# LayerNorm 1 of a decoder layer with features on the partitions, its input and W_out centred beforehand, its sum of squares by products with ones

## The reference, cut to what matters

```python
proj = x @ w_in                      # 1024 -> 512 pooling + 4 x 512 mLSTM + 8 gates
y_pool = ...                         # trailing-window pooling mixer
h, C1, n1, m1 = _mlstm(q, k, v, ig, fg, C, n, m)
y_ml = sigmoid(o_pre) * h
mix = concatenate([y_pool, y_ml], axis=-1) @ w_out
x1 = _layer_norm(ALPHA * x + mix, ln1_g, ln1_b)
ff = square(relu(x1 @ w_ff1 + b_ff1)) @ w_ff2 + b_ff2
x2 = _layer_norm(ALPHA * x1 + ff, ln2_g, ln2_b)

def _layer_norm(x, g, b):
    mu = mean(x, axis=-1)
    xc = x - mu
    var = mean(xc * xc, axis=-1)
    return xc * rsqrt(var + LN_EPS) * g + b
```

## Time and profile before

| | us |
|---|---|
| median of 3 runs | 1066.43 (1066.04 to 1066.63) |
| profiled execution, its span | 1064.2 |
| TensorE busy in it | 1053.9 |
| DVE busy | 724.6 |
| ACT busy | 500.3 |
| GpSimd busy | 92.3 |

### The profile page before, as it was taken

One profiled execution on the slowest core, in us unless ns is written; L12 is line 12 of the kernel. 1 busy time (PEld: TensorE's weight loads), 2 busy tenths in 40 slices (PEclk: granted clock), 3 DMA queues, 4 the chain that ended last, 5 costly groups with the idle time before them and its releaser, 6 DMA issues. The chain is left out here.

```text
span 1064.2 us, 19251 instructions
## 1 busy us (share of the span) xinstructions
PE 1053.9 (99%) x7935; PEld 1042.0 (98%) x7935; DVE 724.6 (68%) x989; ACT 500.3 (47%) x733; POOL 92.3 (9%) x119
## 2 busy tenths in 40 slices
PE   9999999999999999999999999999999999999996
PEld 9999999999899999999999999999999999999985
DVE  6795555537789864955555555558767577788977
ACT  6453535442554666654555545556452322334223
POOL 3010000020212320000000000000000000000027
PEclk9999999999999999999999999999999999999999
DMA  8502222362154841235435534568623525435304
GB/s 283 147 4 60 63 60 63 92 175 79 47 200 127 259 126 46 80 120 170 150 119 159 158 119 154 163 221 275 239 81 139 170 71 167 132 91 169 120 9 151
DMA packets 97394, 139.88 MB, mean 131 GB/s; under 512 B 5963, under 2 KB 56875, under 8 KB 96934
## 3 DMA queue, kind: packets, MB, share of 16 engines
q1 hardware_dynamic: 93728, 127.65, 37.9%
q0 software_dynamic: 3328, 10.77, 3.6%
q10 hardware_dynamic: 270, 0.49, 0.2%
HBM read 102.75 MB, written 36.38 MB: 131 GB/s over the span
## 5 line engine op out<-in xcount | busy, mean ns | idle before, releaser
L2201 PE MATMUL bank<-x_hi,w_hi 128*128 128x344 f32 (+1 forms) x696 | 228.1, 328 | 0.0
L2201 PE MATMUL bank<-x_hi,d_lo 128*128 128x258 f32 x968 | 222.4, 282 | 0.0
L2201 PE MATMUL bank<-x_lo,w_hi 128*128 128x344 f32 (+1 forms) x696 | 222.0, 319 | 0.0
L2201 PE MATMUL bank<-x_hi,w_lo 128*128 128x344 f32 x528 | 168.8, 320 | 0.0
L2201 PEld LDWEIGHTS bank<-x_hi,d_lo 128*128 128x128 f32 x968 | 165.7, 189 | 0.0
L2201 PEld LDWEIGHTS bank<-x_hi,w_hi 128*128 128x128 f32 (+1 forms) x696 | 130.4, 187 | 0.1
L2201 PEld LDWEIGHTS bank<-x_lo,w_hi 128*128 128x128 f32 (+1 forms) x696 | 130.3, 187 | 0.1
L2201 PE MATMUL bank<-x_lo,s_hi 128*128 128x258 f32 x448 | 126.5, 282 | 0.0
L2201 PE MATMUL bank<-x_hi,s_hi 128*128 128x258 f32 x448 | 126.4, 282 | 0.0
L2201 PEld LDWEIGHTS bank<-x_hi,w_lo 128*128 128x128 f32 x528 | 99.2, 188 | 0.0
L2201 PE MATMUL bank<-t_hi,s_hi 128*128 128x258 f32 x336 | 95.2, 283 | 0.0
(11 more groups left out here) (391 smaller groups left out, 2485.2 us busy)
## 6 DMA issues: line engine op xcount, KB each, us to landing
h_ops<-h_unit SPq DMA_DIRECT2D x56, 258.0 KB, 2.8
x_lo_raw<-h_ops SPq DMA_DIRECT2D x14, 1032.0 KB, 5.3
s_raw<-in_w_ff SPq DMA_DIRECT2D x14, 1024.0 KB, 7.0
w_raw<-in_w_out SPq DMA_DIRECT2D x12, 1024.0 KB, 6.9
x_lo_raw<-h_ops SPq DMA_DIRECT2D x14, 774.0 KB, 4.5
d_raw<-in_w_ff SPq DMA_DIRECT2D x9, 1024.0 KB, 7.8
w_raw<-in_w_in SPq DMA_DIRECT2D x16, 512.0 KB, 6.2
h_ops<-t_out SPq DMA_DIRECT2D x28, 258.0 KB, 5.0
```

The costliest lines, as they stand in the source:

```text
L2201: return nc.tensor.matmul(out, lhsT, rhs, start=start, stop=stop, skip_group_check=True)
```

## The change

Let xc be x minus its mean over the features, and Wc be W_out with the mean of each row, over the output features, taken off. Then ALPHA * xc + h @ Wc equals ALPHA * x + h @ W_out minus its own mean. The change computes that sum, so that the mean of LayerNorm 1 is zero, and keeps features on the partitions throughout.

- **The mean of x.** A column of −1/1024 is put into the padding of the gate product, whose row 68 then holds minus the mean of each token. SP writes it to DRAM (`nm_d`).
- **x centred in DRAM** (`xt_d`). SP writes the high parts of x at units 4 and 5. GpSimd adds the low parts at pairs 7 and 8, and minus the mean in eight broadcasts at pairs 10 and 11; these DMAs add to what is in DRAM. SP loads each row of 128 features (`load_xt`) in the output stage.
- **W_out centred.** GpSimd loads W_out's rows at pairs 2 to 5, two of 128x1024 at a time; DVE sums each along its row (`w_out_rows`, in four pairs, at units 4 and 5). ACT adds minus the mean to each quarter of W_out before its split (`centre`, eight instructions a quarter).
- **Order of the output products** (`OUT_ORDER`, written (j, b)). Each quarter of W_out is loaded and split once. The 24 products are numbered p, two for each entry.
- **The residual** (`residual(p)`): DVE adds ALPHA times xc while it evacuates the product, in place of ACT's copy.
- **The variance.** ACT squares a block's outputs (six, then two chunks), TensorE makes eight fp32 products of a matrix of ones with the squares (`square_sums(b)`), which gives the sum on all partitions. ACT takes the root, DVE the reciprocal and two multiplications over 4x344, ACT scales and shifts and makes the high part in two halves, DVE the low parts.
- `mix_T`, `norm_T`, `norm1`, `ln1_a`, `ln1_b`, `x1_T`, `mix_evac` and GpSimd's nine loads of x by tokens are gone.

The diff, without the removed functions, which the listing above shows:

```diff
-U_FFN = U_OUT + NBLK * (D // UW)
+U_FFN = U_OUT + D // UW
+OUT_ORDER = [(0, 0), (1, 0), (0, 1), (1, 1), (0, 2), (1, 2), (2, 0), (3, 0), (2, 1), (3, 1), (2, 2), (3, 2)]
...
+                if u == 3:
+                    sp.wait_ge(x_hi, 2 * len(XT) + 1 + NBLK)
+                    sp.dma_start(nm_d, GL[NH:NH + 1, 0, :]).then_inc(nm_out, 16)
                 if u >= 3:
                     load_rows(u - 3)
+                if u == 4:
+                    sp.dma_start(xt_d[:, 4:8, :], XH[:, 4:8, :].bitcast(F32)).then_inc(xt_hi, 16)
+                elif u == 5:
+                    for b in (0, 2):
+                        sp.dma_start(xt_d[:, 0:4, blk(b)], XH[:, 0:4, blk(b)].bitcast(F32)).then_inc(xt_hi, 16)
+                    sp.wait_ge(b12_out, 48)
+                    sp.dma_start(xt_d[:, 0:4, blk(1)], b12_d[0]).then_inc(xt_hi, 16)
...
+            def load_xt(m):
+                if m == 0:
+                    sp.wait_ge(xt_done, XT_DONE)
+                    sp.wait_ge(pooled, 4)
+                elif m == 1:
+                    sp.wait_ge(sn_out, 16)
+                elif m == 2:
+                    sp.wait_ge(E_ready, 2 * NPAIR)
+                    sp.wait_ge(qi_ready, NPAIR)
+                elif m == 3:
+                    sp.wait_ge(mixed, 12)
+                else:
+                    sp.wait_ge(gemm_read, outputs_of(m - 4, m - 3, NBLK - 1))
+                sp.dma_start(XTM[:, 3 - m % 4, :], xt_d[:, m, :]).then_inc(xt_in[m % 4], 16)
...
+                    p = PAIRS * h + j
+                    if 2 <= p < 6:
+                        if p == 2:
+                            pool.wait_ge(dve_row, ROW_RX)
+                            pool.wait_ge(act_row, 6)
+                        else:
+                            pool.wait_ge(wr_sum, 2 * (p - 2))
+                        for x in range(2):
+                            k = 2 * (p - 2) + x
+                            pool.dma_start(WR[x][:, :], a["w_out"][0, P * k:P * (k + 1), :]).then_inc(wr_in, 16)
+                    elif p == 7:
+                        pool.wait_ge(xt_hi, XT0 + 64)
+                        pool.dma_start(xt_d[:, 4:8, :], XL[:, 4:8, :].bitcast(F32), max_dma_last_dim=4 * NT, accum_op=ALU.add).then_inc(xt_done, 16)
+                    elif p == 8:
+                        for b in (0, 2):
+                            pool.dma_start(xt_d[:, 0:4, blk(b)], XL[:, 0:4, blk(b)].bitcast(F32), max_dma_last_dim=4 * NT, accum_op=ALU.add).then_inc(xt_done, 16)
+                        pool.dma_start(xt_d[:, 0:4, blk(1)], b12_d[1], max_dma_last_dim=4 * NT, accum_op=ALU.add).then_inc(xt_done, 16)
+                    elif p in (10, 11):
+                        if p == 10:
+                            pool.wait_ge(nm_out, NM0 + 16)
+                            pool.wait_ge(xt_done, XT_LO)
+                        for k in range(4 * (p - 10), 4 * (p - 10) + 4):
+                            pool.dma_start(xt_d[:, k, :], nm_d.to_broadcast([P, NT]), max_dma_last_dim=4 * NT, accum_op=ALU.add).then_inc(xt_done, 16)
...
+            def centre(j):
+
+                u = U_OUT + j
+                act.wait_ge(raw_in[u % 2], RAW_AT[u])
+                if j == 0:
+                    act.wait_ge(wr_sum, KC + 1)
+                for k in range(KC):
+                    A(wslot(RAW, u)[:, k, :], wslot(RAW, u)[:, k, :], ACT.Identity, bias=WM[:, k:k + 1]).then_inc(w_centred, 1)
...
+            def square(b, last):
+                m0, m1 = (6, 8) if last else (0, 6)
+                act.wait_ge(gemm_read, outputs_of(m0, m1, b))
+                if not last:
+                    if b == 0:
+                        act.wait_ge(c_out, 128)
+                    else:
+                        act.wait_ge(var_ready, VAR0 + b)
+                A(SQ[:, m0:m1, :], Y[:, m0:m1, blk(b)], ACT.Square).then_inc(squared, 1)
+
+            def root(b):
+                act.wait_ge(var_ready, VAR0 + b + 1)
+                if b:
+                    act.wait_ge(ln_norm, 2 * b)
+                A(RSTD[:, :], D_[:, 0:BLK], ACT.Sqrt, scale=1.0 / D, bias=EPSC).then_inc(ln_sqrt, 1)
...
+            def x1_half(b, h):
+                act.wait_ge(ln_norm, 2 * b + h + 1)
+                ks = slice(4 * h, 4 * h + 4)
+                for f in range(4 * h, 4 * h + 4):
+                    A(Y[:, f, blk(b)], Y[:, f, blk(b)], ACT.Identity,
                       scale=CST[:, G1 + f:G1 + f + 1], bias=CST[:, B1 + f:B1 + f + 1]).then_inc(xv_ready, 1)
+                act.wait_ge(xv_ready, KC * b + 4 * h + 4)
+                A(XH[:, ks, blk(b)], Y[:, ks, blk(b)], ACT.Copy).then_inc(x1_hi, 1)
+
+            square(0, False)
+            square(0, True)
+            root(0)
+            square(1, False)
+            x1_half(0, 0)
+            x1_half(0, 1)
+            square(1, True)
+            root(1)
+            ffn_hi(0)
+            square(2, False)
+            x1_half(1, 0)
+            square(2, True)
+            ffn_hi(1)
+            root(2)
+            x1_half(1, 1)
...
+            def w_out_rows(u, i):
+                if u in (4, 5) and i in (2, 5):
+                    for x in range(2):
+                        k = 4 * (u - 4) + 2 * (i // 3) + x
+                        dve.wait_ge(wr_in, 32 * (k // 2 + 1))
+                        V.tensor_reduce(WM[:, k:k + 1], WR[x][:, :], AX.X, ALU.add).then_inc(wr_sum, 1)
+                    if (u, i) == (5, 5):
+                        dve.wait_ge(wr_sum, KC)
+                        V.tensor_scalar(WM[:, :], WM[:, :], -1.0 / D, None, ALU.mult).then_inc(wr_sum, 1)
...
+            def residual(p):
+                j, b = OUT_ORDER[p // 2]
+                m, n = 2 * j + p % 2, N_PROJ + p
+                dve.wait_ge(gemm_done, n + 1)
+                if b == 0:
+                    dve.wait_ge(xt_in[m % 4], XT0 + 16 * (m // 4 + 1))
+                stt(Y[:, m, blk(b)], XTM[:, 3 - m % 4, blk(b)], ALPHA, bank[n % 3][:, 0:BLK], ALU.mult, ALU.add)\
+                    .then_inc(gemm_read, 1)
...
+            def r_std(b):
+                dve.wait_ge(ln_sqrt, b + 1)
+                V.reciprocal(RSTD[:, :], RSTD[:, :]).then_inc(ln_rstd, 1)
+
+            def normed(b, h):
+                dve.wait_ge(ln_rstd, RSTD0 + b + 1)
+                r = Y[:, 4 * h:4 * h + 4, blk(b)]
+                V.tensor_tensor(r, r, over_blocks(RSTD[:, :], 4), ALU.mult).then_inc(ln_norm, 1)
+
+            def x1_lo_half(b, h):
+                dve.wait_ge(x1_hi, 2 * b + h + 1)
+                ks = slice(4 * h, 4 * h + 4)
+                V.tensor_tensor(XL[:, ks, blk(b)], Y[:, ks, blk(b)], XH[:, ks, blk(b)].bitcast(F32),
...
+            residual(5)
+            cat_lo_part(2, False)
+            residual(6)
+            sample_rows()
+            residual(7)
+            cat_lo_part(2, True)
+            residual(8)
+            new_C(0)
+            residual(9)
+            split_lo(U_OUT + 2)
+            residual(10)
+            new_C(1)
+            residual(11)
+            split_lo(U_OUT + 3)
+            residual(12)
+            residual(13)
+            residual(14)
+            residual(15)
+            residual(16)
+            r_std(0)
+            residual(17)
+            normed(0, 0)
+            normed(0, 1)
+            residual(18)
+            residual(19)
+            x1_lo_half(0, 0)
+            residual(20)
+            x1_lo_half(0, 1)
+            r_std(1)
+            residual(21)
+            normed(1, 0)
+            normed(1, 1)
+            ffn_lo(0)
+            residual(22)
+            residual(23)
+            x1_lo_half(1, 0)
...
+            def square_sums(b):
+                pe.wait_ge(squared, SQ0 + 2 * b + 2)
+                if b:
+                    pe.wait_ge(ln_sqrt, b)
+                else:
+                    pe.wait_ge(nat_read, 2)
+                for m in range(KC):
+                    last = mm(D_[:, 0:BLK], ONES[:, :], SQ[:, m, :], m == 0, m == KC - 1)
+                last.then_inc(var_ready, 1)
...
+                elif p == 16:
+                    square_sums(0)
+                elif p == 20:
+                    square_sums(1)
...
+                if i == 0:
+                    square_sums(2)
```

More of the change, by code:

```diff
@@ L189, in build_layer @@
         o_xn = o_fa + 2 * XROW + 4 * HALF * 4
-        XN = at("x_nat", [P, 2, D], o_xn)
-        RS = at("res_nat", [P, 2, D], o_xn + 8192)
+        XTM = at("x_T_centred", [P, 4, NT], R["h_blk"])
+        SQ = at("squares", [P, KC, BLK], R["qkv0"] - 3 * XROW)
+        RSTD = at("r_std", [P, BLK], R["sample_C"])
+        WR = [at(f"w_out_rows{x}", [P, D], o_r1 + (6 + x) * XROW) for x in range(2)]
         o_top = [o_r2, o_r2 + 2 * TOP, o_xn]
@@ L1762, in variance, with scale_and_shift @@
                 V.tensor_scalar(L[:, 14:15], L[:, 13:14], EPS, None, ALU.add).then_inc(stats, 1)
-            def scale_and_shift(t, sqrt_done, numbers, tiles=TILES):
+            def scale_and_shift(t, sqrt_done, numbers, tiles):
                 L = LNT[0:tiles[t][1], t % 3, :]
```

(55 more changed lines are left out.)

245 lines of the change are left out of this document (71 added, 174 removed).

## The result

The changed kernel takes 1081.67 us in the median (1079.02 to 1082.21, 4 runs) against 1066.51 of before (4 runs, one more than in the table above): a ratio of 1.0139, 95% interval 1.0124 to 1.0153. The forecast was 1066.9, its range 1064.9 to 1071.9. The profiled execution is the one of 1081.15 us, with a span of 1079.4, 15.2 more than the earlier trace rows.

A forecast was written before the change was run, and what follows sets the result against it. TensorE, busy for 1053.9 of 1064.2 us, was taken as the bound. The terms −0.7 + 0.4 + 0.3 + 0.5 = +0.5 gave a span of about 1064.7 and a time of 1066.9 us, range 1064.9 to 1071.9.

The forecast's parts named there:

- rival C: Slower: the accumulating transfers of x and the mean's broadcasts could delay a weight transfer by some us; about 1070, chance 0.04.
- TensorE's own account: Output product and LayerNorm 1: 15.0 us off for removed transposes, 14.3 on for ones products; −0.7, between −1.0 and −0.3.
- p = 8: First product of the output stage's third block: TensorE waits for the last low parts, +0.4 us (0.2 to 0.6).
- Row sums of W_out: Vector-engine reductions, units 4 and 5: +0.3 us (0 to 0.6) for both pairs, +0.5 (0 to 6) for late rows.
- Rival A: Slower: W_out's rows land late in unit 4, holding the vector engine and TensorE; 1072.4 at 13.9 us landing, chance 0.14.
- The chain of LayerNorm 1: Squares, root, reciprocal, scale and shift have cover and cost nothing; margin 1.3 us at the second block's squares.
- Rival B: Slower: LayerNorm 1's scale and shift take 0.8 instead of 0.46 each, so squares come late; about 1069.5, chance 0.08.
- Rival D: Faster: ones products run like split ones, 0.157 each, 3.8 instead of 14.3 us; time 1056.4, chance 0.03.

## Why the prediction was wrong, step by step

**The step that failed is rival C.** It said of the adding transfers that "they would have to be 60 us late to be waited for; their load could delay a weight transfer by some us", gave about 1070 and a chance of 0.04; the sum itself has no term for these transfers at all. The first half asks when the transfers' own result is read, and is true, though the second four were issued at 218 us and not by 215. The second half was left as a guess, though the trace of before could have answered it: which loads are issued in that stretch, after how long do they land, and how long after their issue are they needed. The reload of x_lo had 19 us from issue to its use and took 6.1; the last w_in load was issued at 222.35, just as the engines became 0.88 busy, and the scalar engine reached its split 14.5 us later:

```profile
236.83 1.91 ACT L807 ACTIVATE w_hi<-w_raw 128x2048 fp32r<-128x2048 f32 x1
```

It then took 5.2 to land, and 28.5 with the broadcasts in front. The price was 15 us (10.2 idle, 4.4 slow clock), nearly five times the 3 that I gave. The trace of before shows these covers, but not how late a load would be; that the range should have reached past 1080 is hindsight.

**The clock.** I priced each stall at its own length. Here each of the two idle stretches of 5.8 and 4.4 us was followed by 4.0 and 4.8 us at the 1.2 GHz level, which added 4.4 to 10.2. That was not in the sum. Shorter stalls did not pay it: the one of 1.3 us in the run with pairs 8 and 9, and one of 1.9 us at 167 us in the run with pairs 7 and 8, left the granted clock of their stretches at 1.00. Between 1.9 and 4.4 us nothing was measured.

**TensorE's own account: right in kind, some tenths too small.** −15.0 and +14.3 gave −0.7. The ones blocks cost 4.6 each, 13.9 in all; the earlier trace rows gave 4.8 each. In the run with the late broadcasts TensorE is busy for 1053.0 us against 1053.9; by the account below it is about −1.4.

**p = 8: right.** 0.4 was forecast; the changed kernel's timeline has 0.22 of idle time:

```profile
334.64 0.43 PE L2315 MATMUL bank<-x_hi,w_hi 128*128 128x344 f32 x1 [0.22 <-DVE x_lo L1612]
```

Idle time counts from the end of the matmul before, whose record lasts 0.32 while the next one normally starts after 0.16. By starts, the two steps from 334.10 to 334.90 took 0.80 instead of 0.32: 0.48 lost.

**Row sums of W_out: right.** The vector and tensor engines in unit 4, where the earlier trace rows were read before:

```profile
110.29 2.34 DVE L1715 TENSOR_REDUCE w_out_means<-w_out_rows 128x1 f32<-128x1024 f32 x2 [0.52 <-DMA w_out_rows<-in_w_out]
...
115.68 0.51 DVE L1678 SCALAR_TENSOR_TENSOR y_acc<-bank,y_acc 128x344 f32<-128x344 f32 x1
```

```profile
116.33 0.40 PE L2315 MATMUL bank<-t_rows_b_r,w_hi 128*128 128x344 f32 x1 [0.37 <-DVE y_acc L1678]
```

A pair takes 2.3 us; the rows landed 0.5 after they were wanted, which I had taken as the value; the vector engine is 2.7 late at the addition and TensorE waits 0.37 where 2.27 were covered, 0.6 by starts. Unit 5 has no listed wait, but 0.2 by starts at the same product. Together that is 0.8, and 0.3 for two pairs and 0.5 for the wait were forecast. Rival A did not happen. The Trainium skill ("DMA: Bandwidth & Descriptors", the SWDGE path) would have had these rows land 4.4 us after issue; the first pair took 8.4 in the median here, beside other transfers, and my 8.5 from the rows held. The three later pairs, with little else on the DMA engines, took 4.2 to 4.4, as the page has it; so its figure holds here for a pair alone. The Trainium skill ("DMA: Bandwidth & Descriptors", the section on queues, rings and completion order) says that the engines alternate between queue rows by packet. The run with the transfers at pairs 7 and 8 agrees, with 629 and 627 packets in the stretch, and shows what it means: packets of 3.6 KB against 0.5, so nearly all of the time goes to GpSimd's queue.

**The chain of LayerNorm 1: right, with half the margin.** There is no wait at the squares or the first feed-forward products. Scale and shift start 0.57 us apart where I had used 0.46, and the second block's last squares end at 385.82, its ones products start at 386.48: a margin of 0.7 instead of 1.3. In the run with late broadcasts and rounded ones the two times are 367.25 and 367.90, the same margin: rounded ones make the cover shorter and start the chain earlier by the same amount, so that run is no harder test of it. Rival B is out; it needed 0.8.

**Rival D: wrong as put, right as a price.** Plain fp32 ones products cost what the earlier trace rows said. Rounded ones cost 0.157 each, and gave the 10 us that D named.

**The account of the 15.2 us.** Compare the starts of the same TensorE steps, the transposes of `h_nat`, in the kernel before and then in the changed one. Behind both stalls:

```profile
254.72 0.38 PE L2205 MATMUL bank<-identity,h_nat 128*128 128x128 f32 x2
```

```profile
270.37 0.38 PE L2319 MATMUL bank<-identity,h_nat 128*128 128x128 f32 x2
```

The changed kernel is 15.65 late there. At the last such step before the stalls (226.84 and 227.71) it is 0.87 late, from units 4 and 5. So the two stalls with their slow clock cost 14.8. From 280.24 and 295.87 to the first feed-forward product of halves (437.60 and 452.29) it gains 0.94, with the 0.48 of p = 8 in it. The last 0.5 lies behind TensorE's last product, where the two executions take 7.6 and 8.1 us.

**What stays open.** No run moved fewer bytes at pairs 10 and 11, or issued them on SP's queue. From what length on a stall costs slow clock is open between 1.9 and 4.4 us. The 0.5 us at the end has no cause shown.

## What to carry to other kernels

A transfer that a change adds has two readers: the one who waits for its data, and the one whose load shares the engines with it. List every load that is issued in the stretch behind it, with its landing and the time of its first use, and put new bulk traffic where the next needed load is far, not where the DMA engines look idle at the moment of issue or simply earlier. Column sums with ones on TensorE are worth having once the operands are rounded; in plain fp32 they cost here nearly as much (13.9 us) as the 18 blocks of transposes that they replaced (15).

## What the runs showed of the hardware

- Eight GpSimd-issued transfers of 516 KB: 8.4 us to landing as plain broadcasts from DRAM, 9.4 as sums from SBUF, 12.2 to 12.3 as adding broadcasts.
- With GpSimd's queue full, loads of SP's of 512 KB took 30.2 us to land; in 15 us the two queues moved 629 and 627 packets, but 2.26 and 0.32 MB; in the changed kernel, in 21.5 us, 761 and 750 packets, but 3.80 and 0.82 MB.
- After 5.8 and 4.4 us of idle TensorE the granted clock was 0.50 for 4.0 and 4.8 us of work; after 1.3 and 1.9 us it stayed at 1.00.
- A reduction of 128x1024 on the vector engine takes 1.21 us; a product of 128x128 by 128x344 with ones takes 0.545 in plain fp32 and 0.157 rounded.
